# A two-layer hybrid decoder step: sample attention four steps later, the first query tile drops its 12 lowest keys, index dots in pairs of heads

## What is computed

```python
def indexer_scores(qi, wi, ki):
    dots = jnp.einsum('bqhd,bsd->bqhs', qi, ki).astype(jnp.float32) * (D_IDX ** -0.5)
    w = wi.astype(jnp.float32) * (N_IDX_HEADS ** -0.5)
    return jnp.einsum('bqh,bqhs->bqs', w, jax.nn.relu(dots))
...
        sc = indexer_scores(qi_b, wi_b, ki)
        adm = key_pos[None, :] <= q_pos[:, None]
        sc = jnp.where(adm[None], sc, -jnp.inf)
        _, idx = lax.top_k(sc, top_k)      # top_k = 528 // 4 = 132
```

## Time and profile before

| | |
|---|---|
| median of 3 runs | 876.19 us (873.66 to 878.19) |
| profiled execution | 876.71 us |
| its span | 875.4 us |
| PE busy | 805.3 us (92%) |
| DVE busy | 609.3 us (70%) |
| ACT busy | 328.0 us (37%) |
| POOL busy | 333.1 us (38%) |
| mean granted clock of PE | 0.945 |

### The profile page before, as it was taken

How to read it: one execution, slowest core, us unless ns; L and a number is a source line. 1 busy time by engine, 2 the same in 40 slices (tenths; PEclk the granted TensorE clock), 3 DMA queues, 4 the chain that set the end, 5 groups by cost and what they waited for, 6 DMA issues and landing times. The chain is left out here.

```text
span 875.4 us, 13288 instructions
## 1 busy us (share of the span) xinstructions
PE 805.3 (92%) x4620; PEld 637.6 (73%) x4620; DVE 609.3 (70%) x1432; ACT 328.0 (37%) x830; POOL 333.1 (38%) x317
## 2 busy tenths in 40 slices
PE   5898989999889899999998899899998889999998
PEld 4894635568767777789998655455877777678998
DVE  3546997999998974433444879989999898531122
ACT  3735335336653331223132444343484524122102
POOL 0033886934744700110110568886274373000000
PEclk9999989999889998999999999999999899799999
DMA  4533040314143633012134304002414154400212
GB/s 166 154 99 100 16 121 13 84 42 124 49 113 94 203 124 123 1 44 81 61 101 113 100 4 121 24 21 83 144 52 106 53 163 143 144 1 23 71 54 98
DMA packets 57283, 75.09 MB, mean 86 GB/s; under 512 B 13233, under 2 KB 32889, under 8 KB 57185
## 3 DMA queue, kind: packets, MB, share of 16 engines
q1 hardware_dynamic: 57106, 74.17, 27.7%
q10 hardware_dynamic: 111, 0.08, 0.0%
HBM read 67.26 MB, written 7.61 MB: 86 GB/s over the span
## 5 line engine op out<-in xcount | busy, mean ns | idle before, releaser
L1164 PE MATMUL R<-x_hi,W_r 128*128 128x268 f32 x448 | 141.1, 315 | 27.2 <-DVE yT L1668 7.9
L1148 PE MATMUL R<-W_r,x_hi 128*128 128x512 f32 (+3 forms) x320 | 127.8, 399 | 12.2 <-DVE W_r L1474 12.2
L1177 PE MATMUL R<-yT,W 128*128 128x268 f32 (+2 forms) x768 | 135.0, 335 | 2.4 <-DVE yT L1474 2.4
L1166 PE MATMUL R<-x_hi,W_r 128*128 128x268 f32 x448 | 136.0, 304 | 0.0
L1165 PE MATMUL R<-x_lo,W_r 128*128 128x268 f32 x448 | 135.7, 303 | 0.0
L1177 PEld LDWEIGHTS R<-yT,W 128*128 128x128 f32 x768 | 114.8, 201 | 16.0 <-DVE yT L1474 2.6
L1149 PE MATMUL R<-W_r,x_hi 128*128 128x512 f32 (+3 forms) x320 | 120.7, 377 | 0.0
L1164 PEld LDWEIGHTS R<-x_hi,W_r 128*128 128x128 f32 x448 | 92.2, 206 | 38.9 <-DVE yT L1668 11.9
L1150 PE MATMUL R<-W_r,x_lo 128*128 128x512 f32 (+3 forms) x320 | 120.3, 376 | 0.0
L1474 DVE SCALAR_TENSOR_TENSOR cc<-uext,params,cc 128x528 f32<-128x528 f32 x120 | 110.4, 965 | 0.0
L764 POOL TENSOR_TENSOR W_r<-W,W_r 128x1024 fp32r<-128x1024 f32 x28 | 66.4, 2380 | 88.8 <-ACT W_r L882 88.6
(11 more groups left out here) (232 smaller groups left out, 1408.5 us busy)
## 6 DMA issues: line engine op xcount, KB each, us to landing
W<-in_w_in SPq DMA_DIRECT2D x52, 512.0 KB, 4.2
KV<-in_cache_k SPq DMA_DIRECT2D x32, 256.0 KB, 2.8
W<-in_w_out SPq DMA_DIRECT2D x8, 1024.0 KB, 7.4
KV<-in_cache_v SPq DMA_DIRECT2D x32, 256.0 KB, 2.8
ubx<-qkv_rows SPq DMA_DIRECT2D x16, 256.0 KB, 3.7
zi<-z_rows SPq DMA_DIRECT2D x16, 196.0 KB, 3.6
W<-in_w_in SPq DMA_DIRECT2D x8, 296.0 KB, 3.4
out_new_k_prompt<-kz SPq DMA_DIRECT2D x8, 256.0 KB, 2.0
```

What stands on the lines that cost most here:

```text
L1148: pe.matmul(out, x_hi[:, kc, rows], hi, start=(kc == 0), stop=False)
L1164: pe.matmul(out, hi[:, cols], x_hi[:, kc, toks], start=(kc == 0), stop=False)
L1166: m = pe.matmul(out, lo[:, cols], x_hi[:, kc, toks], start=False, stop=(kc == KC - 1))
L1177: m = pe.matmul(R[:, k, 0:hi - lo], W[:, slot(x), kc % 4, 128 * (u[1] % 4):128 * (u[1] % 4) + 128], yT[:, kc, lo:hi], start=(kc == 0), sto ...
```

## The change

Three things change.

*Selection.* Tile 1 has 144 keys, so keeping 132 is dropping 12. The scores of tile 1 are copied negated and in reverse order into an area `LOW` of `bias`, with four sentinels of their own that POOL sets; two rounds (`LOW_ROUNDS`) take out the sentinels and the 12 lowest, and the threshold is written back. Tiles are now advanced one instruction at a time by `select(i)`: `early()` advances tiles 1 and 2, twice behind each piece and tap of k tile 4 and of q; `late()` advances tiles 3 and 4 by one round at each n not in `NO_ROUND`, from which 7 and 20 are taken out. The three rounds before item 0 are gone. Each tile has its own slot in `m8` and waits on its own last step.

*Index dots.* `PIECES` goes by pairs of heads; `dots(first)` makes two pieces in a row, behind every twelfth chunk matmul and no longer one behind every sixth.

*Samples.* All of `SX` from `pages` on moves by four steps. PV takes four pages a step in four steps. SP issues the first two output weight loads between page loads.

```diff
+LOW = SENT + WIDTH[1] + 12
+LOW_ROUNDS = (WIDTH[1] - TOPK_P + SENT) // 8
...
-PIECES = [(i, h, a, b) for pair in ((1, 2), (3, 4)) for h in range(IH) for i in pair
-          for a, b in ([(0, WIDTH[i])] if WIDTH[i] <= 512 else [(0, WIDTH[i] // 2), (WIDTH[i] // 2, WIDTH[i])])]
+PIECES = [(i, h, a, b) for pair in ((1, 2), (3, 4)) for two in range(0, IH, 2) for i in pair
+          for a, b in ([(0, WIDTH[i])] if WIDTH[i] <= 512 else [(0, WIDTH[i] // 2), (WIDTH[i] // 2, WIDTH[i])])
+          for h in (two, two + 1)]
...
-NO_ROUND = (7, 9, 10, 12, 16, 18, 20)
-ROUNDS_EARLY = 3
+NO_ROUND = (9, 10, 12, 16, 18)
...
-SX = {"pool_diff": 9, "pool_diff2": 10, "ln_diag": 12, "ln_mul": 16, "ln_tanh": 17, "pages": 18, "swish": 20, "index": 26,
-      "index_turn": 27, "topk": 28, "logits": 32, "exp": 33, "norm": 34, "turn": 35, "keep": 36, "pv": 37, "ahead": 41, "gate": 45}
+SX = {"pool_diff": 9, "pool_diff2": 10, "ln_diag": 12, "ln_mul": 16, "ln_tanh": 17, "pages": 22, "swish": 20, "index": 30,
+      "index_turn": 31, "topk": 32, "logits": 36, "exp": 37, "norm": 38, "turn": 39, "keep": 40, "pv": 41, "ahead": 41, "gate": 45}
...
-            for m in range(30, 34):
-                w_load(m)
+                if b == 2:
+                    w_load(30)
+                    w_load(31)
+            w_load(32)
+            w_load(33)
...
+            misc0.did(pool.memset(bias[:, 0, LOW:LOW + SENT], BIG))
...
-                    if first_dots is not None and kc % 2:
-                        dots(first_dots + kc // 2)
+                    if first_dots is not None and kc % 4 == 3:
+                        dots(first_dots + kc // 4 * 2)
...
-                if p >= 2:
-                    pe.wait_ge(*rel_s.at(p - 1))
...
+                else:
+                    pe.wait_ge(*rel_s.at(first))
...
-                if SX["pv"] <= n < SX["pv"] + 8:
+                if SX["pv"] <= n < SX["pv"] + 4:
...
-                    for g in range(2):
-                        page = 16 + 2 * b + g
+                    for page in range(16 + 4 * (n - SX["pv"]), 20 + 4 * (n - SX["pv"])):
+                        b, g = divmod(page - 16, 2)
...
+            def select(i):
+
+                k, best = steps_of[i], m8[0:ROWS[i], slot_of[i], :]
+                field, n = (low, LOW_ROUNDS) if i == 1 else (area(i), ROUNDS)
+                k -= i == 1
+                if k > 2 * n + 1:
+                    return
+                if i in mark:
+                    dve.wait_ge(*tk_s.at(mark[i]))
+                if k < 0:
+                    tk_s.did(dve.tensor_scalar(flipped, area(1, SENT), -1.0, None, ALU.mult))
+                elif k == 2 * n:
+                    if i == 1:
+                        tk_s.did(dve.tensor_scalar(area(1, SENT), flipped, CUT, NEG, ALU.is_lt, ALU.mult))
+                    else:
+                        tk_s.did(dve.tensor_scalar(area(i), area(i), CUT, NEG, ALU.is_gt, ALU.mult))
+                elif k == 2 * n + 1:
                     causal(i, tk_s)
+                elif k % 2 == 0:
+                    tk_s.did(dve.max(best, field))
+                else:
+                    tk_s.did(dve.match_replace(field, best, field, GONE))
+                steps_of[i] += 1
+                mark[i] = tk_s.n
...
                     piece(p)
                     p += 1
+                    if i == 4:
+                        early()
                     if x < TAPS_K[i]:
                         tap(j)
                         j += 1
+                    if i == 4:
+                        early()
...
-                if i < 4:
-                    topk_round((1, 2))
...
-            for _ in range(NT + 2, ROUNDS):
-                topk_round((1, 2))
-            to_bias((1, 2))
-            tb12 = tk_s.n
...
-                more_topk(n)
-                if n == 22:
-                    assert rounds[0] == ROUNDS
-                    to_bias((3, 4))
-                    tb34 = tk_s.n
+                if n < 5:
+                    select(2)
+                if n not in NO_ROUND:
+                    late()
```

More of the change, by code:

```diff
@@ L1250, in kq_turn, with dots @@
                 kqt_s.did(m)
-            def dots(p):
-                i, h, lo, hi = PIECES[p]
-                if p == 0:
+            def dots(first):
+                if first == 0:
                     pe.wait_ge(*idxk_s.at(NT))
-                if p >= 2:
-                    pe.wait_ge(*rel_s.at(p - 1))
-                b = 32 * (h % 4)
-                ix_s.did(pe.matmul(A[0:ROWS[i], p % 2, 0:hi - lo], qkT[b:b + 32, h // 4, START[i]:START[i] + ROWS[i]],
-                                   qkT[b:b + 32, 2, lo:hi], start=True, stop=True))
+                else:
+                    pe.wait_ge(*rel_s.at(first))
+                for p in (first, first + 1):
+                    i, h, lo, hi = PIECES[p]
+                    b = 32 * (h % 4)
+                    ix_s.did(pe.matmul(A[0:ROWS[i], p % 2, 0:hi - lo], qkT[b:b + 32, h // 4, START[i]:START[i] + ROWS[i]],
+                                       qkT[b:b + 32, 2, lo:hi], start=True, stop=True))
             p = 0
@@ L1502, in vector_layer @@
             dve.wait_ge(*st_t.at(2))
-            dve.wait_ge(*misc0.at(3))
+            dve.wait_ge(*misc0.at(4))
             def tok(h):
@@ L1545, in causal @@
                 s.did(dve.tensor_tensor(d, d, tri[0:ROWS[i], 0:ROWS[i]], ALU.add))
[L1547 to L1551, removed]
-                for x, i in enumerate(pair):
-                    dve.wait_ge(*tk_s.at(tk_s.n - 1))
-                    tk_s.did(dve.match_replace(area(i), m8[0:ROWS[i], x, :], area(i), GONE))
@@ L1556, in to_bias @@
[L1556 to L1563 removed]
+            steps_of, mark, slot_of = {1: 0, 2: 0, 3: 0, 4: 0}, {}, {1: 1, 2: 0, 3: 0, 4: 1}
+            low = bias[:, 0, LOW:LOW + SENT + WIDTH[1]]
+            flipped = bias[:, 0, LOW + SENT + WIDTH[1] - 1:LOW + SENT - 1:-1]
@@ L1565, in vector_layer, with early, late @@
+            def early():
+                select(1)
+                select(2)
+            def late():
+                for _ in range(2):
+                    select(3)
+                    select(4)
             n1 = sum(1 for q in PIECES if q[0] <= 2)
@@ L1647, in vector_layer @@
                 conv_s.did(dve.tensor_scalar(cc[:, c, NTOK:TOK], wsum[:, c, :], prm[:, 10 + c:11 + c], None, ALU.add))
-            for _ in range(NT + 2, ROUNDS):
-                topk_round((1, 2))
-            to_bias((1, 2))
-            tb12 = tk_s.n
-            rounds = [0]
-            def more_topk(n):
-                if rounds[0] < ROUNDS and n not in NO_ROUND:
-                    topk_round((3, 4))
-                    rounds[0] += 1
             def gate(g):
@@ L1668, in gate_in @@
                 evD.did(dve.tensor_tensor(yT[:, ch, tok(u[2])], R[:, bank(u), 0:HALF], row[:, tok(u[2])], ALU.mult))
-            for _ in range(ROUNDS_EARLY):
-                more_topk(0)
             def take(u):
```

15 lines of the change are left out of this document (6 added, 9 removed).

## The result

The changed kernel takes 893.1 us (median of 4 runs, 890.97 to 895.57) where the kernel before takes 875.86 (4 runs): a ratio of 1.0192, with a 95% interval of 1.0142 to 1.0241. The forecast was 877.0 with a range up to 888; the time lies outside, on the slow side.

What follows compares the result with a forecast made beforehand. DVE was taken to pace the k stage and the first half of the items. Front +3.7, items -3.7 and tail +0.4 made +0.4 a layer, +0.8 on 876.7, less 0.5 for the median: 877.0 us, range 866 to 888.

Steps and rivals of the forecast that it cites:

- The weight loads ahead of the page loads: SP's queue in the items: two 1 MB loads ahead of pages cost 0; without cover, one page late by at most 7.3 us.
- Tail +0.4: End of the layer: index operation at step 30 and values four pages a step, +0.4 us a layer, from -3 to +3.
- one long and one short drop: +4.0 for -3.5: Steps 41 to 44: half-clock drops behind the values' tiny matmuls cost 4.0 us a layer in place of 3.5.
- rival B: Steps 41 to 44: four-page blocks halve the clock at each step, +4 us more a layer, 885 us; chance 0.12.
- s18 to s28, -6.0: Scores 18 to 28: pages four steps later bring DVE's load below PE's 41.9 us, PE's gaps close, -6.0 us.
- Round at item 7, +2.3: First half of the items, paced by DVE: an early round made up at item 7 adds 2.3 us.
- Front +3.7: Stages k, q and v before the items: selection there starts v 3.0 us later, cooling adds 0.7; from +1 to +5.5 a layer.
- Rest(14): Weight split after k tile 4's selection: ends 3.0 us later (4.9 - 0.9 - 1.0); PE's wait of 4.07 becomes about 7.
- Pairs: Index dots in k and q: a pair saves 0.27 us, counting only where PE is late, eight of 20 pairs a layer.
- The new wait for ACT: Paired index dots wait until ACT has read both banks: taken at 0, at most 0.63 us each if ACT is late.
- Rival C: Front free since DVE's q stage has room, item gain stays: -3.3 us a layer, 870; 866 with dots side by side; chance 0.28.
- Rival A: Selection in k and q paid in full: front +6.0, items gain only 2.0, +4.4 us a layer, 885.5; chance 0.20.

Runs made afterwards that it cites:

- select_in_v: w_late with the selection of tiles 1 and 2 wholly in the v stage, three rounds before item 0 again, none at items 7, 20, 21; 863.97 us, ratio 0.9838.
- select_q_only: w_late without selection steps in k tile 4; they follow in q, the rest of tile 2 in the v stage; 874.32 us, ratio 0.9963.
- select_only: The kernel before with the new selection alone, sample attention where it was; 892.29 us, ratio 1.022.
- pairs_only: The kernel before with the index dots in pairs of heads alone, with the new wait for ACT; 882.06 us, ratio 0.9983.
- no_shift: Pairs of dots and selection in the v stage as in select_in_v, but sample attention where it was before the change; 874.41 us, ratio 0.9982.
- w_late: The changed kernel with all four output weight loads behind the last K page again; 880.44 us, ratio to before 0.9989.
- values_quarter: w_late with one of four column groups of each V page multiplied, leaving out three quarters of the samples' value sums; 845.47 us in two runs.

## Why the prediction was wrong

The forecast's sum was +0.4 us a layer, and the layers grew by 9.5 and 10.1. Two of its terms failed: the weight loads, taken at 0, and the clock behind the blocks of values.

- **The weight loads ahead of the page loads** were taken at 0, with the cover named (two steps ahead) and 7.3 us as the price without it. The cover isn't there: the price was 6.2 us in each layer, 12.5 of the 17 us. The step failed by counting the depth of the page queue in steps and not in bytes. Behind 2 MB on full DMA engines even the 196 KB of index rows come too late, and POOL, not PE's step, sets when they are wanted.
- **Tail +0.4** was +7.1 and +7.3 from s30 to the end. The step that failed is "one long and one short drop: +4.0 for -3.5". In layer 0 of the changed kernel four stretches at half clock stand in and just behind the steps of the values, 10.2, 6.8, 6.8 and 3.4 us long, and cost 13.6; in the kernel before there are three of 3.4 in layer 0 (from 383.9, 394.1 and 428.2), and one of 6.9 in layer 1. That is rival B's mechanism, at more than its price. The baseline excuses little: from s30 to values the kernel before took 101.6 and 103.2 us in the trace that was read, 101.6 to 106.4 in the other two, and the changed kernel 108.7 and 108.8. Why drops come in one execution and not in the next stays open.
- **s18 to s28, -6.0**: -6.2 in both layers. Right, and for the stated reason: POOL is busy 15.56 and not 27.36 us, DVE 36.93 and not 46.85 (the sum had it at 40 and 44), PE 41.73 of 41.73. The threshold pair takes 0.72 us.
- **Round at item 7, +2.3**: s9 to s18 grew by 3.1 and 1.6, and without the round (select_in_v against select_q_only) it is 3.1 and 2.7 shorter. Right.
- **Front +3.7**: items started 0.6 us earlier in layer 0 and 1.2 later in layer 1; against the cheaper layers of the kernel before (131.0 from k0 to item 0's scores) it is +1.1. The place was right and the sizes were not. Rest(14) was to come 3.0 later and came 2.0 later: the selection alone makes 3.3 (4.0 in the sum), the pairs -1.6 (-1.0). Pairs give 0.65 each and not 0.27. The wait is 8.68 where about 7 was said, since PE reaches it 2.7 us sooner. From there to item 0 the sum kept all of the delay and added 0.7; measured, 1.1 of the 2.0 is left, and select_only's 3.3 becomes 2.3 to 3.0, so that without pairs the selection in q costs nothing more. That DVE sets the pace of the k stage mostly stands: the pairs made PE's part of it 2.8 us shorter in pairs_only, and then PE waited 2.0 us longer for rest(14). The matmul at 120.09, called k tile 4, is already one of q tile 0, and PE's k stage ends at 118.5.
- **The new wait for ACT** was taken at 0, with 0.63 as the most that one could cost, and is 13.2 us in 14 waits, the longest 2.1 (2.3 in 4 before, of the same line). It eats up a part of what the pairs save.
- **Rival C** had two things right: dots side by side, and front and items together, -3.7 and -3.4 us a layer where it had -3.7. It took the loads and the tail as the forecast did, and missed by them. **Rival A** did not come true: rest(14) ends less than its 4 us later, the front costs less than its 6.0, and the items gained in full at s18 to s28.

## What to carry to other kernels

A large load put ahead of small ones that an engine needs soon can cost nearly its whole transfer, here 6.2 us for 2 MB: count the bytes on the queue, not the steps. A stage whose length varies from trace to trace at constant length times granted clock must be read from several traces before a change is measured against it. And selection or other work with slack belongs in the stage where nobody waits for its engine, here the v stage, even where another stage shows idle time on that engine.

## What the hardware showed

Two matmuls of 32 rows on neighbouring row groups take the time of one (0.66 against 0.65 us at 272 columns). Identical work in s36 to values took 59.6 to 66.3 us in one and the same kernel, by the granted clock alone (0.94 to 0.85). pairs_only and no_shift, which come to it some microseconds earlier, took 66.3 us in all four layers and so gained in the front and not in the time; whether coming earlier is the reason isn't shown. Half clock in the steps of the values goes away when a quarter of their tiny matmuls is left (13.6 us in w_late, none in values_quarter).
